# The delta rule's solve on TensorE: a block-diagonal state, two heads to one product

## The chip, the cores and the metric

One NeuronCore of a Trainium2 chip. The metric is device time of one launch in microseconds (us). The kernel before took 1455.86 us, the median of three runs (1449.7, 1455.86 and 1456.06).

## The reference, cut to what matters

A network of several blocks on 256 tokens in float32: feed-forward stages, mixers and gates. The change is inside one mixer, the `hyb` stage, which runs a stick-breaking attention (8 heads of 64) beside an RWKV-7 recurrence (8 heads of 64). Per head the recurrence is a delta rule with decay, over tokens t:

```
S_t = S_{t-1} * w_t  +  (S_{t-1} a_t) b_t^T  +  v_t k_t^T      (S is 64 x 64 for a head)
y_t = S_t r_t
```

The kernel computes it in two chunks of 128 tokens (c = 0, 1). With decays folded into A, R (queries of the removal and of the output), B and K (keys), it forms four 128 x 128 triangular matrices G for each head and chunk, and inverts (I - G0) in levels into Y. Then for each chunk:

```
right sides  rs = A S + G2 v          (S is zero in chunk 0, so the first term is left out there)
unknowns     us = Y rs
outputs      y  = R S + G1 us + G3 v
next state   S  = (B^T us + K^T v) * decay          (after chunk 0 only)
```

## The kernel before, in words

Each engine has its own instruction stream, written out by hand; an engine's instructions run in the order written, and semaphores (`signal(...)`, `.inc`, `.at`, `wait_ge`) order the engines among one another. Nothing is scheduled by a planner. `ps` is the PSUM tensor: 8 banks of 128 partitions x 512 float32. Everything in the solve is float32, and each float32 product appears in the profile as two records of MATMUL and two of LDWEIGHTS, so "x16" is eight products.

Two heads share a tile of 128 partitions: head 2j has partitions 0 to 63 and head 2j+1 partitions 64 to 127 of `AR[:, j]` (A and R, features first) and of the state `s0` (128 x 4 x 64). A product with the state therefore has 64 rows of stationary operand, `64*128` in the profile; products with G or Y have 128 rows, `128*128`.

TensorE's part of the solve (program order, after the seven levels of the inverse, L1393 to L1427):

- `rhs(0)` (L1365, eight products of 64 columns), `stick_scores(2)` (L1295, L1296), `unknowns(0)` (L1372), `stick_scores(3)`,
- `next_state` (L1379, L1380): for each head two products whose stationary operand has 64 columns, into partitions 0 to 63 or 64 to 127 of bank 7 (`128*64`),
- `outputs(0)` in two halves (L1388, L1389), `stick_sums(2)` between them (L1303, L1304, which wait for GpSimd's `softplus(2)`),
- a wait for the state and for the kept outputs of chunk 0, then `rhs(1)` in two halves (L1364 with the state, then L1365, for each head in turn), `stick_sums(3)` between and after them, `unknowns(1)`, `stick_out(2)` (L1313, L1314),
- `outputs(1)` two heads at a time (L1387 with the state, then L1388, L1389), each time followed by a quarter of the output gate: L1419 with 128 rows, L1420 with 32; `stick_out(3)` before the third quarter,
- `project_rows("hyb_out")` (L1034), four weight chunks; ahead of the third `turn_y` (L1433) transposes the normed outputs, and VectorE makes the second half of its input (L2713, L2716).

Even heads write bank 4 and odd heads bank 5, at columns `hd // 2 * 64`, for right sides and outputs alike. ScalarE keeps them with two ACTIVATEs of 256 columns (`keep_by_parity`, L1927) and the unknowns with one of 512 (L1932). VectorE makes the state from bank 7 with one instruction (L2687), ahead of `stick_softplus(2)` (L2660) in its queue; GpSimd masks what that makes (`softplus`, L2147). Later ScalarE, VectorE and GpSimd norm the outputs of each chunk (L2698 to L2705, L1947, L2101).

Weights come through six bays (L724); a bay is loaded again once TensorE has signalled that it is done with it. The gate's two chunks are released after L1420's last product, and their bays take the first weights of the next stage, `conv0`.

Of the kernel before, what the change touches and what calls it, by code (L numbers as in the profile page):

```python
# [11 lines left out]
ALU = mybir.AluOpType  # L12
ACT = mybir.ActivationFunctionType
AX = mybir.AxisListType

P = 128
# [201 lines left out]
def build(nc, I, scratch, out, book):  # L218
    new = {}
    ctx = ExitStack()  # L220
    with ctx:
        def sb(name, shape, dt=F32):
            return ctx.enter_context(nc.sbuf_tensor(name, shape, dt))

        def signal(name):
            return Signal(ctx, nc, name, book, new)
# [281 lines left out]
        at = at_k  # L508
        X, at = carve(at, 4, 4, P)
        Y, at = carve(at, 4, 4, P)  # L510
        rs, _ = carve(at - 2048 - 2048, 2, 4, 64)
        us, _ = carve(at - 2048 - 2048 + 512, 2, 4, 64)
        yv, _ = carve(at - 2048 - 2048 + 1024, 2, 8, 64)
        qaT, at = carve(at, 4, SEQ)
        kaT, at = carve(at, 4, SEQ)
# [6 lines left out]
        vtok = sq_flat[:, 0:1024].rearrange("p (t n) -> p t n", t=TT)  # L522
        bktok = sq_flat[:, 1024:2048]
        btok, ktok = bktok[:, 0:512], bktok[:, 512:1024]
        s0 = sb("state", [P, 4, 64])
        sfac = sb("state_decay", [P, 4])
        gmean = sb("group_mean", [P, 16])
        rw_in = signal("rwkv_projection_kept")
# [13 lines left out]
        sol_p = signal("solve_by_tensor")  # L542
        sol_a = signal("solve_by_scalar")
        sol_d = signal("solve_by_vector")
        LEVEL_N = len(LEVELS)
        STICK_BANK = [4, 6, 0, 2]

# [3 lines left out]
        def head(t, hd):  # L551

            return t[64 * (hd % 2):64 * (hd % 2) + 64, hd // 2]
# [212 lines left out]
        def _(pe):  # L766
            def weights(key, i=None):

                c = chunks[key]
                count = 16 * (c // BAYS + 1)  # L770
                pe.wait_ge(landed[c % BAYS].sem, count if i is None else i * 16 + count)
# [426 lines left out]
            def hyb():  # L1198
# [155 lines left out]
                level(5)  # L1354
                level(6)

                def cols64(b, hd):
                    return ps[:, b, hd // 2 * 64:hd // 2 * 64 + 64]

                def rhs(c, heads):  # L1360
                    for hd in heads:
                        o, vv = cols64(4 + hd % 2, hd), vtok[:, c, hd * 64:(hd + 1) * 64]
                        if c:
                            nc.tensor.matmul(o, head(AR, hd)[:, c, 0], head(s0, hd), start=True, stop=False)  # L1364
                        mm = nc.tensor.matmul(o, G[:, c, hd, 2], vv, start=(c == 0), stop=True)  # L1365
                    if 7 in heads:
                        mm.then_inc(*sol_p.inc("rhs", c))

                def unknowns(c):
                    pe.wait_ge(*sol_a.at("rhs", c))  # L1370
                    for hd in range(8):
                        mm = nc.tensor.matmul(ps[:, 6, (hd % 2 * 4 + hd // 2) * 64:(hd % 2 * 4 + hd // 2 + 1) * 64],  # L1372
                                              Y[:, c * 2 + hd // 4, hd % 4], rs[:, hd % 2, hd // 2], start=True, stop=True)
                    mm.then_inc(*sol_p.inc("u", c))

                def next_state():
                    for hd in range(8):
                        o = ps[64 * (hd % 2):64 * (hd % 2) + 64, 7, hd // 2 * 64:hd // 2 * 64 + 64]
                        nc.tensor.matmul(o, btok[:, hd * 64:(hd + 1) * 64], us[:, hd % 2, hd // 2], start=True, stop=False)  # L1379
                        mm = nc.tensor.matmul(o, ktok[:, hd * 64:(hd + 1) * 64], vtok[:, 0, hd * 64:(hd + 1) * 64], start=False, stop=True)  # L1380
                    mm.then_inc(*sol_p.inc("state"))

                def outputs(c, heads):
                    for hd in heads:
                        o = cols64(4 + hd % 2, hd)
                        if c:
                            nc.tensor.matmul(o, head(AR, hd)[:, c, 1], head(s0, hd), start=True, stop=False)  # L1387
                        nc.tensor.matmul(o, G[:, c, hd, 1], us[:, hd % 2, hd // 2], start=(c == 0), stop=False)  # L1388
                        mm = nc.tensor.matmul(o, G[:, c, hd, 3], vtok[:, c, hd * 64:(hd + 1) * 64], start=False, stop=True)  # L1389
                    if 7 in heads:  # L1390
                        mm.then_inc(*sol_p.inc("y", c))

# [9 lines left out]
                outputs(0, range(4, 8))  # L1402
                stick_sums(2, 1)
                pe.wait_ge(*sol_d.at("state"))
                pe.wait_ge(*sol_a.at("y", 0))
                rhs(1, range(4))
                stick_sums(3, 0)
                rhs(1, range(4, 8))
# [190 lines left out]
        def _(act):  # L1599
# [229 lines left out]
            def hyb():  # L1829
# [91 lines left out]
                level(5)  # L1921
                level(6)

                def keep_by_parity(dst, *event):
                    act.wait_ge(*sol_p.at(*event))
                    for n in range(2):
                        ins = nc.scalar.activation(dst(n), ps[:, 4 + n, 0:256].rearrange("p (a b) -> p a b", a=4), ACT.Copy)  # L1927
                    ins.then_inc(*sol_a.inc(*event))

                def keep_unknowns(c):  # L1930
                    act.wait_ge(*sol_p.at("u", c))
                    nc.scalar.activation(us[:].rearrange("p a b c -> p (a b c)"), ps[:, 6], ACT.Copy).then_inc(*sol_a.inc("u", c))  # L1932

                def keep_outputs(c):
                    keep_by_parity(lambda n: yv[:, c].rearrange("p (a b) e -> p b a e", b=2)[:, n], "y", c)

                keep_by_parity(lambda n: rs[:, n], "rhs", 0)
                stick_exponentials(2)
                keep_unknowns(0)
                stick_logs(2)  # L1940
# [8 lines left out]
                keep_by_parity(lambda n: rs[:, n], "rhs", 1)  # L1949
                squares_of_outputs(0)  # L1950
                stick_weights(3)
                keep_unknowns(1)
# [130 lines left out]
        def _(pool):  # L2083
# [45 lines left out]
            def hyb():  # L2129
# [75 lines left out]
        def _(dve):  # L2205
# [363 lines left out]
            def hyb():  # L2569
# [112 lines left out]
                for k in range(KD):  # L2682
# [222 lines left out]
```

## Time and profile before

| | us |
|---|---|
| median of three runs | 1455.86 |
| lowest, highest | 1449.70, 1456.06 |
| the profiled execution | 1451.71 |
| its span | 1450.0 |
| TensorE busy in it | 1391.6 |
| mean granted clock | 0.987 |

Times in the profile count from the span's start. PE is TensorE's matmuls, PEld its weight loads, DVE VectorE, ACT ScalarE, POOL GpSimd, SP SyncE; L1364 is line 1364 of the kernel. PEclk is the granted TensorE clock: 1.00 is 2.4 GHz, 0.50 is 1.2 GHz. A MATMUL's recorded duration contains its latency, so successive ones overlap; what one costs in a stream is read from starts, or from the chain of waits. The solve after the inverse stands between 811.7 and 854 us.

### The profile page before, as it was taken

The numbers are of one execution on the slowest core, as the hardware profiler recorded it, in microseconds if no ns is written. First come the engines' busy times: TensorE is split into PE (matmuls) and PEld (weight loads), VectorE is DVE, ScalarE is ACT, GpSimd is POOL, SyncE is SP. The second block draws the span as 40 slices with busy tenths as digits, with TensorE's granted clock in tenths as the row PEclk, the third lists the DMA queues.
The fourth block names the chain that finished last, engine by engine and source line by source line (L and its number), as shares of the span: only waits on it lengthen the run. The fifth ranks groups of instructions, "written<-read, shape, count | busy, mean of one in ns | idle before, by whom it ended". The sixth has DMA issues, their size and how long they took to land.

```text
span 1450.0 us, 25626 instructions
## 1 busy us (share of the span) xinstructions
PE 1391.6 (96%) x10812; PEld 1322.6 (91%) x10812; DVE 896.5 (62%) x1191; ACT 612.0 (42%) x727; POOL 158.9 (11%) x149
## 2 busy tenths in 40 slices
PE   8999999899999999999999999999989999999997
PEld 8999999798899999888889879999988778999997
DVE  5766676674357665732485417877776774777675
ACT  5443454443134554421323522444454473444444
POOL 0000001141000000601020010000051060000023
PEclk9999999999999999999999979999999999999998
DMA  8555745332345555433410024555543503555530
GB/s 340 186 192 198 244 162 189 121 128 77 145 174 175 202 196 188 167 105 111 151 62 1 2 87 159 183 188 197 202 146 115 201 1 117 175 204 189 191 142 29
DMA packets 34744, 218.99 MB, mean 151 GB/s; under 512 B 4259, under 2 KB 6732, under 8 KB 9452
## 3 DMA queue, kind: packets, MB, share of 16 engines
q1 hardware_dynamic: 31888, 215.59, 41.9%
q10 hardware_dynamic: 2780, 2.30, 0.5%
q8 instruction: 58, 0.95, 0.3%
q14 instruction: 18, 0.15, 0.0%
HBM read 216.68 MB, written 1.06 MB: 150 GB/s over the span
## 4 chain that ended last, share of the span: by engine, by line
PE 81%; DVE 10%; ACT 3%; issue 2%; POOL 1%; DMA 1%; SPq 0%; ACTq 0%; POOLq 0%; DVEq 0%
PE ps L894 35%; PE ps L943 14%; PE ps L1034 6%; PE ps L847 6%; PE ps L1016 2%; DVE weights_second_parts L2330 2%; PE ps L1323 2%; PE ps L1328 1%; PE ps L859 1%; DVE x_second_part L2224 1%; PE ps L831 1%; PE ps L1105 1%; PE ps L1005 1%; ACT weights_first_parts L1641 1%; DMA weight_bays<-in_ffn_in 1%
## 5 line engine op out<-in xcount | busy, mean ns | idle before, releaser
L2330 DVE TENSOR_TENSOR weights_second_parts<-weight_bays,weights_first_parts 128x2048 fp32r<-128x2048 f32 x130 | 296.7, 2289 | 151.2 <-ACT weights_first_parts L1641 151.0
L1641 ACT ACTIVATE weights_first_parts<-weight_bays 128x2048 fp32r<-128x2048 f32 x130 | 249.1, 1924 | 260.9 <-PE ps L894 170.0
L894 PE MATMUL ps<-x_first_part,weights_first_parts 128*128 128x256 f32 x1472 | 197.2, 277 | 4.3 <-DVE weights_second_parts L2330 3.7
L894 PE MATMUL ps<-x_second_part,weights_first_parts 128*128 128x256 f32 x1472 | 196.2, 276 | 0.0
L894 PE MATMUL ps<-x_first_part,weights_second_parts 128*128 128x256 f32 x1472 | 196.0, 276 | 0.0
L894 PEld LDWEIGHTS ps<-x_first_part,weights_first_parts 128*128 128x128 f32 x1472 | 180.1, 192 | 5.7 <-ACT weights_first_parts L1641 2.6
L894 PEld LDWEIGHTS ps<-x_second_part,weights_first_parts 128*128 128x128 f32 x1472 | 180.8, 193 | 0.0
L894 PEld LDWEIGHTS ps<-x_first_part,weights_second_parts 128*128 128x128 f32 x1472 | 180.7, 192 | 0.0
L943 PE MATMUL ps<-hidden_first_part,weights_first_parts 128*128 128x256 f32 x704 | 136.5, 276 | 10.1 <-ACT weights_first_parts L1641 7.5
L943 PE MATMUL ps<-hidden_first_part,weights_second_parts 128*128 128x256 f32 x704 | 136.2, 275 | 0.0
L943 PE MATMUL ps<-hidden_second_part,weights_first_parts 128*128 128x256 f32 x704 | 136.1, 275 | 0.0
L2126 POOL TENSOR_TENSOR weights_second_parts<-weight_bays,weights_first_parts 128x512 fp32r<-128x512 f32 x48 | 68.3, 1457 | 508.1 <-ACT weights_first_parts L1804 508.1
L943 PEld LDWEIGHTS ps<-hidden_first_part,weights_first_parts 128*128 128x128 f32 x704 | 106.8, 192 | 11.1 <-issue 6.1
L943 PEld LDWEIGHTS ps<-hidden_first_part,weights_second_parts 128*128 128x128 f32 x704 | 106.9, 192 | 0.0
L943 PEld LDWEIGHTS ps<-hidden_second_part,weights_first_parts 128*128 128x128 f32 x704 | 106.9, 192 | 0.0
L847 PE MATMUL ps<-xT,weight_bays 128*128 128x256 f32 (+1 forms) x368 | 80.8, 380 | 1.1 <-DVE xT L2294 1.1
L847 PEld LDWEIGHTS ps<-xT,weight_bays 128*128 128x128 f32 (+1 forms) x368 | 68.2, 186 | 12.7 <-ACT embedding L1783 1.3
L1034 PE MATMUL ps<-arena,weight_bays 128*128 128x256 f32 x320 | 69.9, 380 | 3.3 <-DVE arena L2513 1.5
L1034 PEld LDWEIGHTS ps<-arena,weight_bays 128*128 128x128 f32 x320 | 60.6, 190 | 12.3 <-DVE arena L2513 1.9
L2101 POOL TENSOR_TENSOR rstd<-mean_squares,minus_half 128x2 f32<-128x2 f32 (+2 forms) x17 | 15.3, 902 | 483.0 <-DVE mean_squares L2281 396.1
L1657 ACT ACTIVATE arena<-arena 128x512 f32<-128x512 f32 x22 | 14.0, 635 | 92.6 <-DVE arena L2349 92.6
L1629 ACT ACTIVATE arena<-arena 128x512 f32<-128x512 f32 x22 | 13.9, 630 | 68.1 <-DVE arena L2375 68.1
(429 smaller groups left out, 2191.1 us busy)
## 6 DMA issues: line engine op xcount, KB each, us to landing
weight_bays<-in_conv_in SPq DMA_DIRECT2D x44, 1024.0 KB, 4.7
weight_bays<-in_ffn_in SPq DMA_DIRECT2D x42, 1024.0 KB, 4.8
weight_bays<-in_ffn_out SPq DMA_DIRECT2D x22, 1024.0 KB, 4.8
weight_bays<-in_conv_out SPq DMA_DIRECT2D x22, 1024.0 KB, 4.7
weight_bays<-in_mix_in SPq DMA_DIRECT2D x19, 1024.0 KB, 4.8
weight_bays<-in_hyb_in SPq DMA_DIRECT2D x13, 1024.0 KB, 4.8
weight_bays<-in_ple_gate SPq DMA_DIRECT2D x12, 1024.0 KB, 4.7
weight_bays<-in_mix_out SPq DMA_DIRECT2D x4, 1024.0 KB, 5.3
```

What stands on the lines that cost most here:

```text
L831: mm = nc.tensor.matmul(ps[:, b0 + q, j % 2 * SEQ:(j % 2 + 1) * SEQ], w[:, k, j * P:(j + 1) * P], pT[:, n, k], start=(k == 0), stop=(k == 1))
L847: mm = nc.tensor.matmul(dst, lhs(k), xT[:, k] if rhs is None else rhs(k), start=(k == 0), stop=(k == n - 1), **kw)
L859: nc.tensor.matmul(dst[j], w[:, k, j * P:(j + 1) * P], xs[0][:, k], start=(k == 0 and w is hi and not (one_bank and j)), stop=False, skip_ ...
L894: mm = nc.tensor.matmul(dst, w[:, k, j * P:j * P + width], x[:, k], start=(n + k == 0), stop=(n == 2 and k == KD - 1))
L943: mm = nc.tensor.matmul(ps[:, tile // 2, tile % 2 * SEQ:(tile % 2 + 1) * SEQ], w[:, j, tile * P:(tile + 1) * P], in_halves(x[:, g % 2, j]) ...
L1016: mm = nc.tensor.matmul(ps[:, b0 + j // 2, j % 2 * SEQ:(j % 2 + 1) * SEQ], w[k // 2][:, k % 2, j * P:(j + 1) * P], srcT[:, k], start=(k == ...
L1034: mm = nc.tensor.matmul(ps[:, tile // 2, tile % 2 * SEQ:(tile % 2 + 1) * SEQ], w[:, j, tile * P:(tile + 1) * P], srcT(k) if callable(srcT) ...
L1323: mm = nc.tensor.matmul(ps[:, g, i * P:(i + 1) * P], G[:, g // 2, g % 2 * 4 + i, 0], X[:, g, i], start=True, stop=True)
L1641: nc.scalar.activation(hi, raw, ACT.Copy).then_inc(*w_hi_ready.inc(f, g, kind, of - g))
L2101: nc.gpsimd.tensor_tensor(rstd[:, c], msq[:, c], minus_half[:, c], ALU.pow).then_inc(*rstd_ready.inc(*n))
L2126: ins = nc.gpsimd.tensor_tensor(lo[:, part], raw[:, part], hi[:, part], ALU.subtract)
L2330: v.tensor_tensor(lo, raw, hi, ALU.subtract).then_inc(*w_lo_d.inc(f, g, kind, of - g))
```

## The change

The state becomes block-diagonal: `s0` is 128 x 4 x (2 x 64), with head 2j's 64 x 64 block at the upper left of tile j, head 2j+1's at the lower right, and zeros elsewhere, which GpSimd writes once (into the arena, where the inverse's M1 lay; hence its wait for the last level). One product of 128 rows and 128 columns, `from_state`, then serves two heads. Right sides go to bank 4 and outputs to bank 5 with all eight heads side by side, unknowns to bank 6 in the heads' order. Only the first product into a bank has `start=True`. `next_state` takes two heads as stationary operand and two as moving one: 128 x 128 results, of which only the two diagonal blocks are used; VectorE takes them with two instructions of 64 partitions. Each ACTIVATE pair becomes one of 512 columns. The wait for the kept outputs of chunk 0 moves from ahead of `rhs(1)` to ahead of the gate and `outputs(1)`.

```
-        rs, _ = carve(at - 2048 - 2048, 2, 4, 64)
-        us, _ = carve(at - 2048 - 2048 + 512, 2, 4, 64)
+        rs, _ = carve(at - 2048 - 2048, 8, 64)
+        us, _ = carve(at - 2048 - 2048 + 512, 8, 64)
+        s0, _ = carve(14080, RWT, 2, 64)
-        s0 = sb("state", [P, 4, 64])
...
+                def from_state(b, c, n, j):
+                    nc.tensor.matmul(ps[:, b, of_pair(j)], AR[:, j, c, n], s0[:, j].rearrange("p a d -> p (a d)"), start=(j == 0), stop=False,
+                                     skip_group_check=True)
 
                 def rhs(c, heads):
                     for hd in heads:
-                        o, vv = cols64(4 + hd % 2, hd), vtok[:, c, hd * 64:(hd + 1) * 64]
-                        if c:
-                            nc.tensor.matmul(o, head(AR, hd)[:, c, 0], head(s0, hd), start=True, stop=False)
-                        mm = nc.tensor.matmul(o, G[:, c, hd, 2], vv, start=(c == 0), stop=True)
+                        if c and hd % 2 == 0:
+                            from_state(4, c, 0, hd // 2)
+                        mm = nc.tensor.matmul(ps[:, 4, of_head(hd)], G[:, c, hd, 2], vtok[:, c, of_head(hd)], start=(c + hd == 0), stop=True,
+                                              skip_group_check=True)
...
                 def next_state():
-                    for hd in range(8):
-                        o = ps[64 * (hd % 2):64 * (hd % 2) + 64, 7, hd // 2 * 64:hd // 2 * 64 + 64]
-                        nc.tensor.matmul(o, btok[:, hd * 64:(hd + 1) * 64], us[:, hd % 2, hd // 2], start=True, stop=False)
-                        mm = nc.tensor.matmul(o, ktok[:, hd * 64:(hd + 1) * 64], vtok[:, 0, hd * 64:(hd + 1) * 64], start=False, stop=True)
+                    for j in range(RWT):
+                        o = ps[:, 7, of_pair(j)]
+                        nc.tensor.matmul(o, btok[:, of_pair(j)], us[:, 2 * j:2 * j + 2].rearrange("p a d -> p (a d)"), start=(j == 0), stop=False,
+                                         skip_group_check=True)
+                        mm = nc.tensor.matmul(o, ktok[:, of_pair(j)], vtok[:, 0, of_pair(j)], start=False, stop=True, skip_group_check=True)
...
                 def outputs(c, heads):
                     for hd in heads:
-                        o = cols64(4 + hd % 2, hd)
-                        if c:
-                            nc.tensor.matmul(o, head(AR, hd)[:, c, 1], head(s0, hd), start=True, stop=False)
+                        o = ps[:, 5, of_head(hd)]
+                        if c and hd % 2 == 0:
+                            from_state(5, c, 1, hd // 2)
...
                 pe.wait_ge(*sol_d.at("state"))
-                pe.wait_ge(*sol_a.at("y", 0))
                 rhs(1, range(4))
...
                 pe.wait_ge(*sol_a.at("u", 1))
+                pe.wait_ge(*sol_a.at("y", 0))
                 weights("g2")
...  (ScalarE)
+                def keep_rhs(c):
+                    act.wait_ge(*sol_p.at("rhs", c))
+                    nc.scalar.activation(rs.rearrange("p a b -> p (a b)"), ps[:, 4], ACT.Copy).then_inc(*sol_a.inc("rhs", c))
...  (GpSimd, between weights(1) and softplus(2))
+                pool.wait_ge(*inv_p.at("Y", LEVEL_N - 1, 3))
+                nc.gpsimd.memset(s0, 0.0).then_inc(*sol_g.inc("zero"))
...  (VectorE)
-                v.tensor_tensor(s0[:], ps[:, 7, 0:256].rearrange("p (a b) -> p a b", a=4), sfac[:].unsqueeze(2).to_broadcast([P, 4, 64]),
-                                ALU.mult).then_inc(*sol_d.inc("state"))
+                dve.wait_ge(*sol_g.at("zero"))
+                for n in range(2):
+                    r = slice(64 * n, 64 * n + 64)
+                    made = ps[r, 7].rearrange("p (j a d) -> p j a d", j=RWT, a=2)[:, :, n]
+                    ins = v.tensor_tensor(s0[r, :, n], made, sfac[r].unsqueeze(2).to_broadcast([64, RWT, 64]), ALU.mult)
+                ins.then_inc(*sol_d.inc("state"))
```

## Rows read from the trace of the kernel before

**Rows 1.** The page: engines; granted clock in 40 slices; the last chain by engine.

```profile
PE 1391.6 (96%) x10812; PEld 1322.6 (91%) x10812; DVE 896.5 (62%) x1191; ACT 612.0 (42%) x727; POOL 158.9 (11%) x149
...
PEclk9999999999999999999999979999999999999998
...
PE 81%; DVE 10%; ACT 3%; issue 2%; POOL 1%; DMA 1%; SPq 0%; ACTq 0%; POOLq 0%; DVEq 0%
```

**Rows 2.** Windows: stretch, length, busy per engine, PEclk, DMA share, GB/s.

```profile
817.24:818.37 1.13, 1.13 (x34) 1.06 (x32) 0.00 (x0) 1.13 (x1) 0.00 (x0) 1.00 0.00 0
824.98:827.75 2.77, 2.74 (x16) 2.30 (x17) 2.67 (x8) 1.99 (x2) 1.56 (x4) 1.00 0.00 0
828.80:831.55 2.75, 2.75 (x17) 2.27 (x16) 0.00 (x0) 0.00 (x0) 0.00 (x0) 1.00 0.02 6
835.26:837.02 1.76, 1.76 (x14) 1.55 (x13) 0.88 (x1) 0.38 (x1) 1.56 (x3) 1.00 0.00 0
837.02:838.28 1.26, 1.26 (x7) 0.60 (x6) 0.00 (x0) 0.00 (x0) 0.00 (x0) 1.00 0.00 0
840.93:854.18 13.25, 13.25 (x43) 8.49 (x42) 1.24 (x3) 1.04 (x3) 0.00 (x0) 0.50 0.00 0
854.18:857.94 3.76, 3.76 (x10) 3.04 (x10) 1.28 (x4) 0.63 (x1) 1.64 (x1) 0.50 0.66 220
```

**Rows 3.** The chain of waits in time order: start, us, what held it.

```profile
811.93 1.73 PE ps L1365 x16
...
823.83 0.22 PE ps L1389 x2
...
834.53 0.59 PE ps L1313 x4
835.12 0.22 PE ps L1314 x4
...
854.25 15.85 PE ps L1034 x64
...
872.30 7.82 PE ps L1034 x35
```

**Rows 4.** Timeline, TensorE: start, us, engine, line, tiles, shapes, records, [idle before].

```profile
808.20 3.74 PE L1328 MATMUL ps<-arena 128*128 128x128 f32 x32
...
825.70 0.43 PE L1364 MATMUL ps<-state,arena 64*128 64x64 f32 x2
826.07 0.43 PE L1365 MATMUL ps<-squares,arena 128*128 128x64 f32 x2
```

**Rows 5.** Timeline: from the state to the next product that waits.

```profile
818.48 0.42 DVE L2687 TENSOR_TENSOR state<-ps,state_decay 128x256 f32<-128x256 f32 x1 [2.65 <-PE ps L1380]
...
819.34 0.96 DVE L2660 SCALAR_TENSOR_TENSOR arena<-ps,arena 128x768 f32<-128x768 f32 x1 [0.43 <-ACT arena L1892]
...
821.19 0.91 PE L1303 MATMUL ps<-arena,mats 128*128 128x384 f32 x2 [0.82 <-POOL arena L2147]
...
825.38 0.87 POOL L2147 TENSOR_SCALAR_AFFINE_SELECT arena<-arena 128x256 f32<-128x256 f32 x2 [4.24 <-DVE arena L2660]
```

**Rows 6.** Timeline: GpSimd's clearing of 2048 columns, and its last mask.

```profile
735.88 1.81 POOL L2141 MEMSET arena<- 128x2048 f32 x1
...
835.60 1.22 POOL L2147 TENSOR_SCALAR_AFFINE_SELECT arena<-arena 128x256 f32<-128x256 f32 x2
```

**Rows 7.** Timeline: ScalarE's keeps of right sides and of unknowns.

```profile
831.82 0.66 ACT L1927 ACTIVATE arena<-ps 128x256 f32<-128x256 f32 x2 [4.83 <-PE ps L1365]
...
834.57 0.60 ACT L1932 ACTIVATE arena<-ps 128x512 f32<-128x512 f32 x1 [0.87 <-PE ps L1372]
```

**Rows 8.** Timeline: behind the solve, what is late next.

```profile
857.83 0.69 DVE L2705 TENSOR_TENSOR arena<-arena,rstd 128x512 f32<-128x512 f32 x1 [1.75 <-POOL rstd L2101]
...
873.68 6.69 DVE L2330 TENSOR_TENSOR weights_second_parts<-weight_bays,weights_first_parts 128x2048 fp32r<-128x2048 f32 x3
...
886.03 0.46 PE L859 MATMUL ps<-x_first_part,weights_first_parts 128*128 128x256 f32 x1
```

More of the change, by code:

```diff
@@ L544, in build @@
         sol_d = signal("solve_by_vector")
+        sol_g = signal("solve_by_gpsimd")
         LEVEL_N = len(LEVELS)
@@ L1355, in hyb, with of_pair, of_head @@
                 level(6)
-                def cols64(b, hd):
-                    return ps[:, b, hd // 2 * 64:hd // 2 * 64 + 64]
+                def of_pair(j):
+                    return slice(j * P, (j + 1) * P)
+                def of_head(hd):
+                    return slice(hd * 64, (hd + 1) * 64)
+                def from_state(b, c, n, j):
+                    nc.tensor.matmul(ps[:, b, of_pair(j)], AR[:, j, c, n], s0[:, j].rearrange("p a d -> p (a d)"), start=(j == 0), stop=False,
+                                     skip_group_check=True)
                 def rhs(c, heads):
                     for hd in heads:
-                        o, vv = cols64(4 + hd % 2, hd), vtok[:, c, hd * 64:(hd + 1) * 64]
-                        if c:
-                            nc.tensor.matmul(o, head(AR, hd)[:, c, 0], head(s0, hd), start=True, stop=False)
-                        mm = nc.tensor.matmul(o, G[:, c, hd, 2], vv, start=(c == 0), stop=True)
+                        if c and hd % 2 == 0:
+                            from_state(4, c, 0, hd // 2)
+                        mm = nc.tensor.matmul(ps[:, 4, of_head(hd)], G[:, c, hd, 2], vtok[:, c, of_head(hd)], start=(c + hd == 0), stop=True,
+                                              skip_group_check=True)
                     if 7 in heads:
@@ L1371, in unknowns @@
                     for hd in range(8):
-                        mm = nc.tensor.matmul(ps[:, 6, (hd % 2 * 4 + hd // 2) * 64:(hd % 2 * 4 + hd // 2 + 1) * 64],
-                                              Y[:, c * 2 + hd // 4, hd % 4], rs[:, hd % 2, hd // 2], start=True, stop=True)
+                        mm = nc.tensor.matmul(ps[:, 6, of_head(hd)], Y[:, c * 2 + hd // 4, hd % 4], rs[:, hd], start=(hd == 0), stop=True,
+                                              skip_group_check=True)
                     mm.then_inc(*sol_p.inc("u", c))
                 def next_state():
-                    for hd in range(8):
-                        o = ps[64 * (hd % 2):64 * (hd % 2) + 64, 7, hd // 2 * 64:hd // 2 * 64 + 64]
-                        nc.tensor.matmul(o, btok[:, hd * 64:(hd + 1) * 64], us[:, hd % 2, hd // 2], start=True, stop=False)
-                        mm = nc.tensor.matmul(o, ktok[:, hd * 64:(hd + 1) * 64], vtok[:, 0, hd * 64:(hd + 1) * 64], start=False, stop=True)
+                    for j in range(RWT):
+                        o = ps[:, 7, of_pair(j)]
+                        nc.tensor.matmul(o, btok[:, of_pair(j)], us[:, 2 * j:2 * j + 2].rearrange("p a d -> p (a d)"), start=(j == 0), stop=False,
+                                         skip_group_check=True)
+                        mm = nc.tensor.matmul(o, ktok[:, of_pair(j)], vtok[:, 0, of_pair(j)], start=False, stop=True, skip_group_check=True)
                     mm.then_inc(*sol_p.inc("state"))
@@ L1384, in outputs @@
                     for hd in heads:
-                        o = cols64(4 + hd % 2, hd)
-                        if c:
-                            nc.tensor.matmul(o, head(AR, hd)[:, c, 1], head(s0, hd), start=True, stop=False)
-                        nc.tensor.matmul(o, G[:, c, hd, 1], us[:, hd % 2, hd // 2], start=(c == 0), stop=False)
-                        mm = nc.tensor.matmul(o, G[:, c, hd, 3], vtok[:, c, hd * 64:(hd + 1) * 64], start=False, stop=True)
+                        o = ps[:, 5, of_head(hd)]
+                        if c and hd % 2 == 0:
+                            from_state(5, c, 1, hd // 2)
+                        nc.tensor.matmul(o, G[:, c, hd, 1], us[:, hd], start=(c + hd == 0), stop=False, skip_group_check=True)
+                        mm = nc.tensor.matmul(o, G[:, c, hd, 3], vtok[:, c, of_head(hd)], start=False, stop=True, skip_group_check=True)
                     if 7 in heads:
@@ L1922, in hyb @@
                 level(6)
[L1924 to L1928, printed above, removed]
+                def keep_rhs(c):
+                    act.wait_ge(*sol_p.at("rhs", c))
+                    nc.scalar.activation(rs.rearrange("p a b -> p (a b)"), ps[:, 4], ACT.Copy).then_inc(*sol_a.inc("rhs", c))
                 def keep_unknowns(c):
                     act.wait_ge(*sol_p.at("u", c))
-                    nc.scalar.activation(us[:].rearrange("p a b c -> p (a b c)"), ps[:, 6], ACT.Copy).then_inc(*sol_a.inc("u", c))
+                    nc.scalar.activation(us.rearrange("p a b -> p (a b)"), ps[:, 6], ACT.Copy).then_inc(*sol_a.inc("u", c))
                 def keep_outputs(c):
-                    keep_by_parity(lambda n: yv[:, c].rearrange("p (a b) e -> p b a e", b=2)[:, n], "y", c)
-                keep_by_parity(lambda n: rs[:, n], "rhs", 0)
+                    act.wait_ge(*sol_p.at("y", c))
+                    nc.scalar.activation(yv[:, c].rearrange("p a b -> p (a b)"), ps[:, 5], ACT.Copy).then_inc(*sol_a.inc("y", c))
+                keep_rhs(0)
                 stick_exponentials(2)
@@ L1947, in squares_of_outputs @@
                     nc.scalar.activation(ysq[:, c], yv[:, c], ACT.Square).then_inc(*sol_a.inc("squares", c))
-                keep_by_parity(lambda n: rs[:, n], "rhs", 1)
+                keep_rhs(1)
                 squares_of_outputs(0)
```

## The prediction

> **What bounds the kernel now.** I read the page first: TensorE is busy for 1391.6 of 1450.0 us and holds 81% of the chain that ended last, while the next engine, VectorE, is at 62% [rows 1]. So time that leaves TensorE's stream leaves the kernel, unless a wait takes its place. The line of the granted clock has one slice that stands out, a 7 between 834 and 870 us, and that is where the edited code runs. The windows then resolve the solve: until 840.9 us the clock is 1.00; from 840.93 to 857.94 it is 0.50, half rate, although TensorE is busy in all of both stretches [rows 2]. The chain of waits lies on TensorE almost throughout, and it gives what a product costs in a stream: eight products of 64 columns with G take 1.73 us, 0.22 each, and so does a single one in the outputs [rows 3]. The timeline gives two more prices. 16 products of 128x128 by 128 columns take 3.74 us less one latency, again 0.22: a stationary operand of 128 columns costs the same with 64 or with 128 moving columns [rows 4]. And where 64-row products alternate with 128-row ones, each start is 0.37 us behind the last instead of 0.22 [rows 4]: 0.14 to 0.15 us is lost at each change of height.
>
> **Next state: dearer.** Now 16 products with 64-column stationary operands run from 817.24 to 818.37, 1.13 us, or 0.07 each (its x34 are their 32 records and two of the tail ahead) [rows 2]. The new one is 8 products of 128x128 by 128 columns at 0.22: 1.79 us, so +0.65. The least it could be is equal (a change of shape before the outputs falls away, 0.15), the most 8 x 0.37 = 2.9 us, +1.8. VectorE's one instruction of 0.42 us [rows 5] becomes two with the same number of elements per partition on half the partitions: between +0 (both at half the price) and +0.42; I take +0.38, since the elements per partition set the time of all its rows here. The state is then ready near 819.95 instead of 818.91. It stands in VectorE's queue ahead of the second pair's softplus, which began at 819.34 when ScalarE's logarithm came; that moves to about 819.95, and with it GpSimd's mask and the product that waits for it, at 821.19 after 0.82 us of idling [rows 5]. TensorE's own extra 0.65 us falls into that idle time. Cost on the path: **+0.6 us** (bounds 0 and +1.8).
>
> The Trainium skill has a rule that speaks against this edit: "TensorE: Matmul & The Clock Gate", Part 3, says that products of few rows or columns should be placed in different strips of the array, where they run at once. By that rule giving up the 64-column form costs up to half of the throughput here. The trace agrees for next_state, where the 64-column ones stood together (0.07 against 0.22), and the sum above already holds it; for the 64-row ones with the state it has nothing to give, since each stands between two of full height.
>
> **Right sides of chunk 1.** Now two stretches of eight products, 824.98 to 827.75 and 828.80 to 831.55: 5.5 us [rows 2]. New: 4 + 8 products of full height at 0.22, 2.7 us. With the height change into each stretch: **-3.0 us**. Bounds: -1.1 if each still cost 0.37 (12 x 0.37 = 4.4), and -3.2.
>
> **Outputs of chunk 1.** At full clock two heads take 1.76 us (six products, changes of height around the state's) [rows 2]; the new five products take 1.12. Four such: **-2.6 us**. Bounds -0.0 (5 x 0.37 = 1.85 each) and -2.8. The gate's quarters, 1.26 us with a 32-row product that keeps its two changes of height, stay [rows 2].
>
> **The clock.** Before it fell TensorE did just this alternation: 64-row products of 64 columns between full ones, and 32-row products of the gate, all with pauses. It rose again in the dense hyb_out stream [rows 2]. The earlier alternating stretch of the right sides, with the dense sums between, kept 1.00 [rows 2]. The new outputs have neither the 64-row products nor their pauses, and one product in five streams 128 columns; what is left of pauses is two per gate quarter. They are denser than both old stretches, the one that kept the clock too, so I take it that the clock stays. Its worth, by the new stream at full clock: from 835.26 to 854.18 the kernel now needs 18.9 us; new 4 x (1.12 + 1.26) + 0.85 for the last attention product (0.59 + 0.22 and a change [rows 3]) = 10.4 us. That is -8.6, of which -2.6 is counted above: **-6.0 us**. Then the 32 products of hyb_out ahead of the transposes take 15.85 us now; in the second half they run at 7.82 / 35 = 0.2234 us a record, 64 of them in 14.3: **-1.5 us** [rows 3]. Bounds of the clock's part: 0 and -7.5; more in executions in which the clock now falls earlier than in this one.
>
> The skill's same page ("Why this matters for your kernels") ties a throttled clock to idle gaps between bursts of products; [rows 2] show a fall with TensorE never idle. By the page's rule nothing in this change would touch the clock, and the sum would be the first rival's.
>
> **What costs nothing, and its cover.** GpSimd's clearing of 512 columns: 2048 took 1.81 us [rows 6], so 0.45 us (at most 1.8); it can run from 812 on and the next one who needs GpSimd or the zeros comes at 818.5. Cover gone, it is its own 0.45. ScalarE's pair of 0.66 us becomes one of 512 columns, 0.60 [rows 7]; the keep of the right sides is beside the last sums, so nothing, and as little for the outputs. The moved wait: outputs of chunk 0 were kept about when TensorE came, so 0 to -0.2, taken as 0; at its new place the keep is some 7 us old. With a faster TensorE its partners could be late. The softplus mask of the last pair is done at 825.38 + 0.87 = 826.25 [rows 5]; TensorE, started at 825.6 with six products, comes at 826.9: cover 0.7 us, the thinnest here. The right sides' keep is again beside 0.9 us of sums. The last weights' mask stands in GpSimd's queue behind the norm of chunk 0, and that hangs on ScalarE's keep of the new right sides: now the keep ends at 832.48 [rows 7] and the mask at 836.82 [rows 6], 4.3 us later; new the keep ends near 829.8, so the mask near 834.2, and the product that needs it comes at 838. The normed outputs of chunk 1 are ready at 858.5 [rows 8] for transposes at 870.1 [rows 3]; both move. Behind that the loads for conv0 start with the gate's release, so they move along; their parts are split at 880.4, for a first product at 886.03 [rows 8]: 5.6 us of cover, of which 1.5 goes.
>
> **Sum**, against the profiled execution's 1451.71: +0.6 - 3.0 - 2.6 - 6.0 - 1.5 = -12.5, giving 1439.2. The profiled execution lies 4.15 below the median of the runs, 1455.86, from which the same sum gives 1443.4. What separates those runs I can't see; if it is how long the clock was low, the gain is larger in the slow ones. I forecast **1442 us**, chance 0.72, own range 1435 to 1446.
>
> **Rivals.**
>
> *The clock falls all the same* (or falls late in the stretch), chance 0.15. For it: the gate's 32-row products and their pauses stay, and they were in the stretch where it fell. Against: the right sides above. Then only +0.6 - 3.0 - 2.6 = -5.0 is left, 1450.9; with a late fall a few of the 7.5 are kept. I price it 1449, 1445 to 1451.
>
> *The loss isn't one of height.* If every product that follows another operand of another tensor costs 0.37, the bounds above give +1.8 - 1.1 - 0.0 = about +0.7, and some of the clock: 1450 to 1456, chance 0.05. Against: L1388 and L1389 alternate between tensors at 0.22 [rows 3]. This is also the case in which the change doesn't do what it says.
>
> *Slower: the pause ahead of the first sums drops the clock early.* TensorE idles 0.82 us there now [rows 5]; new about 1.0, since the mask comes 0.6 later and outputs(0) start 0.65 later. If the clock fell there and came back only in hyb_out, the new 21 us from 821.8 to 842.9 would take about 18 us more (waits and pauses don't double), and hyb_out 1.5: 1443.4 + 19.5 = 1463. It makes the kernel slower if more than the 12.5 us won are lost, that is if the low stretch begins before about 830. Against: the idle time is nearly the same and dense sums follow it at once. Chance 0.05; the remaining 0.03 is for sizes outside all of these.
>
> **Range and chances.** 0.5%, 7.3 us, is about what a measurement of this kernel can tell from no change. Faster by more than that needs 1448.6 or less: nearly all of 0.72 and half of the first rival's 0.15, and the better half of the rest's: 0.84. Within: 0.11. Slower: 0.05. The 8-in-10 range takes the forecast's own and the first rival's: 1434 to 1451.
>
> **What would show it.** A granted clock of 1.00 from the outputs into hyb_out (rival one: 0.50 in some window there); starts 0.22 us apart in the right sides of chunk 1, two halves of 1.3 us; two heads' outputs in 1.1 us; next_state 1.8 us long and the first sums 0.6 us later against their predecessors; VectorE's state in two instructions near 0.4 us; no idle TensorE before the last pair's sums. The prediction is wrong if the clock is at half rate in the new stretch, or if a new wait for GpSimd's masks stands ahead of the sums or the attention products.

## The result, and the profile after

The changed kernel takes 1441.51 us (median of six, 1440.45 to 1443.64) against 1455.96 for the kernel before (six, 1449.70 to 1456.44). The ratio is 0.9907, 95% interval 0.9894 to 0.9920: 14.45 us faster. The forecast was 1442, range 1434 to 1451.

The profiled execution took 1441.73 us with a span of 1440.0, 10.0 less than before. Windows of the changed kernel (columns as in [rows 2]), answering to [rows 2] and the 15.85 us of [rows 3]:

```profile
819.69:824.51 4.82, 3.78 (x34) 3.64 (x32) 1.80 (x3) 4.78 (x5) 0.77 (x2) 1.00 0.00 0
828.03:829.37 1.34, 1.34 (x15) 1.34 (x14) 1.31 (x4) 1.33 (x2) 0.65 (x2) 1.00 0.00 0
830.24:831.58 1.34, 1.34 (x15) 1.34 (x14) 0.50 (x1) 0.00 (x0) 1.12 (x2) 1.00 0.00 0
835.22:836.33 1.11, 1.11 (x12) 1.11 (x11) 0.70 (x1) 0.38 (x1) 1.11 (x3) 1.00 0.00 0
836.33:837.59 1.26, 1.26 (x7) 0.60 (x6) 0.17 (x1) 0.00 (x0) 0.43 (x1) 1.00 0.00 0
835.22:845.65 10.43, 10.43 (x67) 7.41 (x65) 1.25 (x2) 1.36 (x3) 1.54 (x3) 1.00 0.00 0
845.65:859.57 13.92, 13.92 (x66) 12.22 (x66) 2.72 (x6) 6.26 (x4) 1.64 (x1) 1.00 0.61 227
```

The two halves of the right sides of chunk 1 take 1.34 us each (2.77 and 2.75 before), two heads' outputs 1.11 (1.76), a gate quarter 1.26 as before, all outputs with the gate 10.43 instead of 18.92. PEclk is 1.00 in every one of them, where it was 0.50 for 17 us. hyb_out runs 13.92 us up to its transposes (15.75).

The timeline of the changed kernel, all engines, answering to [rows 5, 6]:

```profile
814.21 1.90 PE L1372 MATMUL ps<-squares,arena 128*128 128x64 f32 x16
...
814.44 0.52 POOL L2172 MEMSET arena<- 128x512 f32 x1 [33.21 <-PE ps L1329]
...
819.69 0.49 PE L1387 MATMUL ps<-arena,squares 128*128 128x128 f32 x2
...
821.58 0.33 PE L1397 MATMUL ps<-arena 128*128 128x64 f32 x2
...
821.77 0.86 DVE L2701 TENSOR_TENSOR arena<-ps,state_decay 64x256 f32<-64x256 f32 x2 [3.49 <-PE ps L1389]
...
822.66 0.96 DVE L2670 SCALAR_TENSOR_TENSOR arena<-ps,arena 128x768 f32<-128x768 f32 x1
...
823.69 0.77 POOL L2155 TENSOR_SCALAR_AFFINE_SELECT arena<-arena 128x256 f32<-128x256 f32 x2 [8.73 <-DVE arena L2670]
...
824.51 0.91 PE L1304 MATMUL ps<-arena,mats 128*128 128x384 f32 x2 [1.04 <-POOL arena L2155]
```

Here is the one part that got dearer. next_state lasts 1.89 us (819.69 to 821.58; 1.13 before), VectorE's two state instructions 0.86 (0.42), and the softplus, which had waited for a logarithm, now follows VectorE's own state at once. From next_state's first product to the first sums it is 4.82 us instead of 3.95. The clearing of the zeros, 0.52 us at 814.44, is in nobody's way.

One measure serves for all kernels below: **the solve**, from the start of chunk 0's first right side to the start of hyb_out's first product, and **the tail**, from there to the start of the transposes. Before: 811.77 to 854.18 and to 869.93, 42.41 and 15.75 us. After: 814.21 to 845.65 and to 859.57, 31.44 and 13.92. Together -12.80. The other 2.8 us of the span's -10.0 went the other way, outside the change: the solve began 2.44 us later, because ahead of the solve the clock fell in places where it hadn't in that execution of the kernel before. These are windows of the changed kernel:

```profile
35.00:40.00 5.00, 3.79 (x20) 3.82 (x21) 4.90 (x5) 1.64 (x3) 0.00 (x0) 0.67 0.51 201
450.00:455.00 5.00, 5.00 (x31) 5.00 (x32) 4.82 (x3) 2.90 (x2) 0.00 (x0) 0.68 0.35 149
610.00:615.00 5.00, 5.00 (x32) 5.00 (x30) 2.54 (x2) 0.00 (x0) 5.00 (x5) 0.66 0.13 23
```

In the kernel before, PEclk is 1.00 in all three of these stretches (it has a fall of its own between 625 and 635 us). Such falls come and go from one execution to the next, so two single executions can't be subtracted; the medians and the local stretches can.

### The profile page after: what moved, and what is told of

Same layout as the page of the kernel before. It is cut to its first block, busy times and chain, and to the rows that moved or that the text cites. A ratio compares the mean times of both kernels' runs of the same rounds, so it can differ in the third digit from the quotient of the medians.

```text
span 1440.0 us, 25560 instructions
## 1 busy us (share of the span) xinstructions
PE 1384.3 (96%) x10780; PEld 1320.8 (92%) x10780; DVE 897.1 (62%) x1192; ACT 611.1 (42%) x723; POOL 159.6 (11%) x150
## 4 chain that ended last, share of the span: by engine, by line
PE 84%; DVE 8%; ACT 3%; issue 2%; POOL 2%; ACTq 0%; POOLq 0%; DVEq 0%
PE ps L895 36%; PE ps L944 15%; PE ps L1035 6%; PE ps L848 6%; PE ps L1017 2%; PE ps L1324 2%; PE ps L1329 1%; PE ps L832 1%; PE ps L860 1%; POOL weights_second_parts L2134 1%; DVE x_second_part L2234 1%; PE ps L1106 1%; ACT weights_first_parts L1650 1%; PE ps L1006 1%; PE ps L1496 1%
```

## The experiments

All medians stand beside medians of the kernel before between 1455.8 and 1456.2 us, measured along with each. The ratio isn't the quotient of the two medians; how sure a difference is, its interval tells.

| kernel | median us (runs) | ratio to before, 95% | solve | tail | low clock in them |
|---|---|---|---|---|---|
| before | 1455.96 (6) | | 42.41 | 15.75 | 840.9 to 857.9 |
| before, again | 1459.41 (1) | | 43.39 | 16.40 | 841.7 to 862.2 |
| after | 1441.51 (6) | 0.9907 (0.9894 to 0.9920) | 31.44 | 13.92 | none |
| after, again | 1441.34 (6) | 0.9896 (0.9875 to 0.9917) | 34.72 | 13.92 | 825.4 to 832.2 |
| outputs by head | 1454.29 (12) | 0.9990 (0.9975 to 1.0005) | 41.27 | 15.98 | 840.3 to 860.7 |
| right sides by head | 1453.57 (12) | 0.9962 (0.9934 to 0.9990) | 46.17 | 16.80 | 835.8 to 866.5 |
| by head, grouped | 1444.46 (6) | 0.9926 (0.9904 to 0.9948) | 32.32 | 13.92 | none |
| before with filler | 1450.65 (12) | 0.9979 (0.9958 to 1.0000) | 39.98 | 13.92 | none |
| before, tails together | 1453.85 (12) | 0.9996 (0.9974 to 1.0018) | 41.94 | 15.41 | 840.8 to 857.8 |
| tails together | 1440.31 (6) | 0.9900 (0.9869 to 0.9930) | 30.17 | 13.82 | none |
| narrow state | 1441.20 (1) | | 30.79 | 13.91 | none |
| both edits | 1438.56 (6) | 0.9894 (0.9863 to 0.9924) | 29.52 | 13.82 | none |
| best | 1439.01 (6) | 0.9911 (0.9872 to 0.9949) | 28.23 | 13.81 | none |
| best, again | 1438.29 (6) | 0.9884 (0.9860 to 0.9908) | 28.24 | 13.81 | none |

The last columns are of the one profiled execution; the ends of a low stretch are read from windows of 1 us.

### The outputs undone

(`by_parity(hd)` is a head's old place: bank 4 for even heads, bank 5 for odd ones.)

```
-                        if c and hd % 2 == 0:
-                            from_state(5, c, 1, hd // 2)
+                        nc.tensor.matmul(by_parity(hd), head(AR, hd)[:, c, 1], s0[64 * (hd % 2):64 * (hd % 2) + 64, hd // 2, hd % 2], start=True, stop=False)
```

> The changed kernel with only the outputs of chunk 1 as before: eight state products of 64 rows, each between products of 128 rows, even heads in bank 4 and odd ones in bank 5. My theory (the changes of height cost 0.14 us each, and their pauses, together with the gate's 32-row products, are what drops the clock): two heads' outputs back from 1.11 to 1.76 us, +2.6 us in all, and a granted clock of 0.50 from somewhere in the outputs into hyb_out, +6 to +7.5: 1450 to 1452 us. Rival (the fall of the clock has nothing to do with the state products' pauses, the change only happened to miss it): +2.6 alone, 1444 us, clock 1.00 in that stretch.

Measured: 1454.29 us, nearly all of the gain gone. Windows of that kernel, the first pair of heads and the low stretch:

```profile
836.26:838.07 1.81, 1.81 (x15) 1.61 (x13) 0.88 (x1) 0.38 (x1) 1.55 (x3) 1.00 0.00 0
840.40:856.52 16.12, 16.12 (x51) 10.58 (x51) 1.24 (x3) 1.04 (x3) 0.00 (x0) 0.50 0.00 0
856.52:860.75 4.23, 4.23 (x11) 3.42 (x11) 1.75 (x4) 0.63 (x1) 1.64 (x1) 0.50 0.72 261
```

Two heads cost 1.81 us again and the clock falls 4 us into the outputs. The fall is tied to the old form of the outputs; the rival is out. The edit brings back the two banks and the two ACTIVATEs too; the grouped kernel below has both of them and kept 1.00, which leaves the products between full ones. It lasted longer than in the kernel before, so the time lies 2 to 4 us above what I expected.

### The right sides undone

```
-                        if c and hd % 2 == 0:
-                            from_state(4, c, 0, hd // 2)
+                        nc.tensor.matmul(by_parity(hd), head(AR, hd)[:, c, 0], s0[64 * (hd % 2):64 * (hd % 2) + 64, hd // 2, hd % 2], start=True, stop=False)
```

> The changed kernel with only the right sides of chunk 1 as before (64-row state products between full ones, two banks, the wait for the kept outputs back ahead of them). My theory: each half back from 1.34 to 2.76 us, +2.9 us in all, clock at 1.00 through the outputs: 1444.5 us. Rival (the clock depends on how sparse the whole solve is, not on the outputs with the gate): the clock falls as in the kernel before, 1451 us.

A miss, and the most telling run. The 12 runs are of two kinds: six between 1442.6 and 1449.6, as I expected, and six between 1457.5 and 1466.3, above the kernel before. The median, 1453.57, lies in the gap between them, where no run is, and the ratio leaves the longest run (1466.27) out. The profiled one (1458.96) is of the second kind; its windows:

```profile
828.48:831.29 2.81, 2.81 (x18) 2.34 (x17) 2.40 (x6) 1.89 (x2) 1.28 (x4) 1.00 0.00 0
832.30:835.12 2.82, 2.82 (x18) 2.35 (x17) 0.00 (x0) 0.00 (x0) 0.00 (x0) 1.00 0.00 0
835.12:835.90 0.78, 0.78 (x5) 0.48 (x5) 0.00 (x0) 0.58 (x3) 0.00 (x0) 0.92 0.00 0
835.90:860.62 24.72, 24.72 (x92) 17.90 (x90) 3.04 (x6) 3.37 (x7) 2.81 (x3) 0.50 0.00 1
860.62:866.50 5.88, 5.88 (x15) 4.71 (x15) 1.80 (x4) 0.63 (x1) 1.64 (x1) 0.50 0.79 297
```

The clock falls right behind the by-head right sides, and then stays at 0.50 through the new, full-height outputs: from 841.21 to 860.62 they take 19.4 us, the same instructions that take 10.43 us in the changed kernel at 1.00. So these outputs can keep a high clock high, but didn't bring a low one back in 19.4 us.

### By head, but grouped

The right sides' part; in the outputs all eight state products stand ahead of the first pair.

```
+                    for hd in heads:
+                        nc.tensor.matmul(by_parity(hd), head(AR, hd)[:, c, 0], s0[64 * (hd % 2):64 * (hd % 2) + 64, hd // 2, hd % 2], start=(hd < 2), stop=False, skip_group_check=True)
+                    for hd in heads:
+                        mm = nc.tensor.matmul(by_parity(hd), G[:, c, hd, 2], vtok[:, c, of_head(hd)], start=False, stop=True, skip_group_check=True)
```

> No block-diagonal product at all: 64-row state products of single heads as before, but standing together (four in a row ahead of each half of the right sides, all eight ahead of the outputs), even heads in bank 4, odd ones in bank 5. My theory (it is the changes of height that cost, not the number of products): 64-row products of alternating halves in a row cost 0.11 to 0.15 us each, so the right sides' half takes about 1.6 us instead of 1.34 and the outputs' stretch about as long as in the changed kernel; clock 1.00; 1442 to 1443 us. Rival (the merging of two heads into one product is what pays): eight products at 0.22 or more, +2 us and more, 1444 to 1446, and 1452 if the clock falls.

Measured: 1444.46 us, with a solve of 32.32, 0.9 over the changed kernel's. The timeline (TensorE) of the grouped kernel:

```profile
829.27 0.66 PE L1382 MATMUL ps<-arena 64*128 64x64 f32 x8
829.86 1.10 PE L1384 MATMUL ps<-squares,arena 128*128 128x64 f32 x8
...
834.45 1.11 PE L1415 MATMUL ps<-arena 64*128 64x64 f32 x16
835.49 0.43 PE L1417 MATMUL ps<-arena 128*128 128x64 f32 x2
```

Eight 64-row products of alternating halves take 1.04 us, 0.13 each, where each took 0.37 between full ones. It is the alternation of heights that cost, and in this execution grouping gives back nearly all that the block-diagonal state gives. It is the shortest of the six, though (1441.12). The median is 3 us above the changed kernel's, its interval overlaps (0.9904 to 0.9948 against 0.9894 to 0.9920), and three of the runs lie between 1446.1 and 1450.8; whether the clock fell in their solve, no trace shows.

### More work in the kernel before

```
                     outputs(1, range(2 * n, 2 * n + 2))
+                    nc.tensor.matmul(ps[:, 1], ident, vtok[:, 0], start=True, stop=True, skip_group_check=True)
```

> The kernel before with four products more, which nobody reads: identity (128x128) by 512 columns into the free bank 1, one behind each pair of heads in the outputs of chunk 1. Each costs about 0.9 us of TensorE at full clock, 3.6 in all. My theory (sparse products dropped the clock): with the stream denser there the clock stays at 1.00 in the outputs, so 1456 + 3.6 - 7.5 = 1452 us: faster with more work. Rival (the fall isn't made by how TensorE is used there): 1460 us, or 1463 with the fillers at half clock.

Measured: 1450.65 us against 1456.03, so not slower with four products more. That it is faster is at the edge of the noise: the ratio's interval, 0.9958 to 1.0000, reaches 1. The profiled execution is the shortest of the twelve, and four of them lie between 1454.7 and 1455.5. What the trace shows is the clock at 1.00 throughout. Its windows, one filler, then the whole of the outputs, then the tail:

```profile
837.61:838.52 0.91, 0.91 (x4) 0.44 (x4) 0.00 (x0) 0.00 (x0) 0.00 (x0) 1.00 0.00 0
835.80:852.29 16.49, 16.49 (x83) 10.53 (x81) 1.98 (x4) 1.43 (x4) 1.55 (x3) 1.00 0.00 0
852.29:866.21 13.92, 13.92 (x66) 12.21 (x66) 2.00 (x4) 6.26 (x4) 1.64 (x1) 1.00 0.61 227
```

This divides the gain, by the local stretches of three single executions. Without fillers and without a fall the old solve would be 39.98 - 4 x 0.91 = 36.34 us. The fall cost 42.41 - 36.34 = 6.1 in the solve and 15.75 - 13.92 = 1.8 in the tail, 7.9; the products' shape gave 36.34 - 31.44 = 4.9.

### Which part of the outputs drops it

The kernel before with the gate's four 32-row products in a row ahead of the outputs:

```
+                for j in range(4):
+                    nc.tensor.matmul(ps[:, 6 + j // 2, j % 2 * SEQ:(j % 2 + 1) * SEQ], wt[:, j * P:(j + 1) * P], xm[0:32, 14],
+                                     start=(j % 2 == 0), stop=False, skip_group_check=True)
```

> The kernel before with only the gate's four 32-row products in a row ahead of the outputs of chunk 1; its state products stay 64 rows high between full ones. It tells the gate's share in the fall of the clock from the state products'. My theory (the state products' pauses suffice): the clock still falls in the outputs, 1454 to 1455 us, only the six changes of height less at half clock. Rival (the gate's small products were needed for the fall): 1.00 in the outputs, 1456 - 7.5 - 0.9 = 1447.5 us.

Measured: 1453.85 us, and 0.50 from 840.8 to 857.8. A window of this kernel, from the fall to hyb_out:

```profile
840.80:854.59 13.79, 13.79 (x50) 10.54 (x50) 0.03 (x1) 1.04 (x3) 0.00 (x0) 0.50 0.00 0
```

So the gate's small products needn't stand between full ones for the fall; the state products do. The small ones still stand in a row ahead of them here, but the same row ahead of the merged outputs ("A better version") left the clock at 1.00.

### The kernel before, once more

> The kernel before once more, to see where the clock falls in another execution. My theory: always within the right sides or outputs of chunk 1, which of the two varies; the earlier it falls, the longer the execution (up to 1460 us; where it doesn't fall, about 1446). Rival (it always falls in the outputs, and the executions differ elsewhere): the fall at the same place within 3 us, relative to the first right side.

It fell in the outputs again, 28.0 us behind the first right side (29.1 in the first profile): the rival's "within 3 us" holds. But the low stretch lasted 20.5 us, not 17, and the two stretches together 59.79 us instead of 58.16. Against the changed kernel's 45.36 that is -14.4. A window of this execution, the low stretch up to hyb_out:

```profile
841.70:857.10 15.40, 15.40 (x49) 9.98 (x49) 1.25 (x3) 1.04 (x3) 0.00 (x0) 0.50 0.00 0
```

The other half of the rival, that executions differ elsewhere, holds as well: the span is 7.7 us longer than in the first profile (1457.7 against 1450.0), and only 1.6 of that lies in solve and tail. My half about the right sides wasn't seen in this kernel; it was seen only with the outputs changed, above.

### The changed kernel, once more

> The changed kernel once more, beside the version with all three edits: 1441.5 us, with no slow tail (1440 to 1444), since in no execution should the clock fall in the solve; the kernel before 1456.

1441.34 us confirms the time, but "in no execution" is refuted. Timeline and then a window of this execution:

```profile
823.29 0.39 PE L1398 MATMUL ps<-squares,arena 128*128 128x64 f32 x2
824.72 1.06 PE L1304 MATMUL ps<-arena,mats 128*128 128x384 f32 x2 [1.05 <-POOL arena L2155]
```

```profile
825.65:832.40 6.75, 6.75 (x30) 6.14 (x29) 3.85 (x8) 3.99 (x5) 0.93 (x3) 0.52 0.00 0
```

TensorE waits 1.05 us for GpSimd's mask, and just behind that the clock is at 0.50; it is back at 832.2, within the new right sides. The solve took 34.72 us instead of 31.44.

### A better version

Three edits on top of the change. First the gate's small products together, as above:

> The changed kernel, with the gate's four 32-row products (128 sigmoid features are in one product, the last 32 in this one) taken out of the quarters and put in a row ahead of the outputs of chunk 1; the full products then add to them. My theory (a change of height costs 0.14 to 0.16 us wherever it is): eight changes become two, a quarter's gate goes from 1.26 to 0.45 us, the four small ones take 1.8 us in a row; -0.9 us in all, and pauses fewer still, so the clock stays at 1.00: 1440.6 us. Rival (four products of 32 rows in a row are the sparsest work of all and drop the clock): 0.50 in the outputs, as in the kernel with the right sides by head, 1455 us.

Solve 30.17 (-1.27; -0.9 expected, so six changes less gave 0.21 each and not 0.15): a quarter's gate product no longer stands between changes of height. In a row the four take 1.9 us (836.39 to 838.31), and the clock stays at 1.00. Then next_state in its old shape, into the diagonal blocks only:

```
+                        o = ps[64 * (hd % 2):64 * (hd % 2) + 64, 7, of_head(hd)]
+                        nc.tensor.matmul(o, btok[:, of_head(hd)], us[:, hd], start=(hd < 2), stop=False, skip_group_check=True)
...
```

> Only next_state in its old form on top of the changed kernel, for the trace. My theory: from the first product of next_state to the first sums 4.2 us instead of 4.8 (before: 3.95). Rival: 4.8, if VectorE's two instructions or the logarithm set it.

Window of this kernel, from next_state's first product to the first sums, 3.98 us (4.2 expected) against 4.82 with two heads to a product:

```profile
819.97:823.95 3.98, 3.13 (x51) 2.93 (x49) 1.80 (x3) 3.95 (x4) 0.77 (x2) 1.00 0.00 0
```

> The same and next_state in its old form of 64-column stationary operands, written into the diagonal blocks only: 16 products in 1.13 us instead of 8 in 1.79. My theory: VectorE's state 0.65 us earlier, the second pair's softplus 0.6 earlier, and with it GpSimd's mask and the first sums; -0.6 us more on top of -0.9: 1440.0 us. Rival: the first sums wait for the chain of ScalarE's logarithm anyhow, 0 for this part.

Solve 29.52, 1438.56 us. And with outputs(0) and rhs(1) no longer cut in halves by the sums, so that four heads' outputs fill the wait for the mask:

```
-                outputs(0, range(4))
+                outputs(0, range(8))
                 stick_sums(2, 0)
-                outputs(0, range(4, 8))
...
-                rhs(1, range(4))
+                rhs(1, range(8))
                 stick_sums(3, 0)
-                rhs(1, range(4, 8))
```

> The version with both edits (gate's small products in a row, next_state in its old form), and now all eight heads' outputs of chunk 0 ahead of the second pair's sums, and all eight heads' right sides of chunk 1 ahead of the last pair's. TensorE idles 1.0 us there now, waiting for GpSimd's mask; my theory: four heads' outputs (1.8 us) fill that idle time, first right side to hyb_out from 29.5 to 28.5 us, 1437.6 us. Rival: the masks come late everywhere, the wait only moves to the last pair's sums, 29.5 and 1438.5 us.

> All three edits again. First right side to hyb_out took 28.23 us against 31.44 in the changed kernel: if the rest of the kernel doesn't give it back, 1441.5 - 3.2 = 1438.3 us; rival: falls of the clock elsewhere take it back, 1441.

Windows of the best kernel: outputs of chunk 0 with both sums' start, the gate's small products, the tail.

```profile
821.44:826.85 5.41, 5.41 (x43) 4.88 (x41) 1.80 (x3) 5.34 (x7) 0.77 (x2) 1.00 0.00 0
833.90:835.82 1.92, 1.92 (x10) 1.40 (x9) 0.87 (x1) 0.38 (x1) 1.92 (x3) 1.00 0.00 0
843.07:856.88 13.81, 13.81 (x65) 12.11 (x64) 3.10 (x6) 6.56 (x5) 1.64 (x1) 1.00 0.62 229
```

The six runs of "best" have their median at 1439.01 us where 1437.6 was expected; the solve of 28.23 is near the 28.5 expected. TensorE is busy in all 5.41 us; the idle time is gone. The solve is 28.23 and 28.24 us in two executions, 3.2 under the changed kernel's, and the medians side by side are 1438.29 and 1441.34. The intervals against the kernel before overlap (0.9860 to 0.9908 and 0.9875 to 0.9917), so the runs alone don't tell these two apart; nor do they tell "both edits" from "best". The traces do.

## Why the prediction was right

The forecast of 1442 us and the sum's local terms both held; the mechanism did too, with three reservations below. Measured on solve and tail against the profiled execution of before:

| step | predicted | measured |
|---|---|---|
| next state, to the first sums | +0.6 | +0.87 |
| right sides, with the changes into them | -3.0 | -2.84 in the two halves alone; -3.31 from the first sums to the unknowns (11.35 to 8.04 us) |
| outputs, shape alone | -2.6 (1.76 to 1.12 for two heads) | 1.76 to 1.11 |
| shape in all | -5.0 | -4.9 |
| clock in the outputs | -6.0 | -6.1 |
| clock in hyb_out | -1.5 | -1.8 |
| sum | -12.5 | -12.80 |

- **Next state** was the term furthest off: I took 1.79 us and 0.38 for VectorE; they measured 1.89 and 0.44 more. The cover I named, the idle time ahead of the sums, did hide TensorE's own part.
- **Changes of height.** The grouped kernel shows it apart: 0.13 instead of 0.37 us for the same products. The Trainium skill says: "Changing tiling mode (not just tile) drains the TensorE" ("TensorEngine Tiling (Array Packing)", Key Properties); the runs agree, with 0.14 to 0.15 us a change here by the starts. That price is low: it sets 0.22 us for a 64-row product, which in a row of its like costs 0.13, and the gate's six changes less gave 0.21 each. My second rival falls with it.
- **The clock.** The filler kernel and the one with the outputs undone confirm the mechanism and, with 7.9 us, its size. The Trainium skill's tie of a throttled clock to idle gaps ("TensorE: Matmul & The Clock Gate", "Why this matters for your kernels") isn't enough here: TensorE was busy throughout ahead of the falls at 840.9 [rows 2] and 835.8, and there denser work, not less idling, kept the clock up. Two small things in this term: 18.9 - 10.4 is 8.5 and not 8.6, and hyb_out's 64 records take 13.92 us at full clock, not 14.3, which is why its part is -1.8 and not -1.5.
- **One reason was weaker than it looked.** I took it as evidence that the old right sides had kept 1.00 [rows 2]. With only the outputs changed, the clock fell behind those same right sides in about half of the runs (if the longer kind is the same thing in all of them: one profile shows it, and the mean granted clock of the runs divides the same way, 0.974 to 0.980 against 0.985 to 0.991). The conclusion held because the change takes the alternation out of both places. With the outputs undone little is left, 1454.3 us; with the right sides undone half of the runs keep nearly all of the gain and half are longer than the kernel before.
- **The first rival** (the clock falls all the same) isn't what was measured in the outputs, in either of the two profiles of the changed kernel.
- **The slower rival** had a wrong price, and its mechanism stays open. The clock did drop behind the longer pause ahead of the first sums, in one of two profiled executions of the changed kernel. Four more kernels have a pause of 1.04 or 1.05 us there and kept 1.00 behind it in their profiles, so it isn't shown that the pause is the cause. And the clock came back within 7 us instead of staying low to hyb_out, so it cost 3.3 us and not 19.5.
- **The covers** held: no TensorE idling ahead of the last pair's sums, GpSimd's zeros 7 us early, and conv0's first product came 16.09 us behind the transposes (859.57 to 875.66), as before (869.93 to 886.03).
- **The median.** The sum from the profile gave 1439.2, from the median 1443.4, and 1442 was a choice between the two; that it lies 0.5 us from the measured 1441.51 is partly luck. Both starting points were off. Outside solve and tail the spans of the 14 profiled executions are between 1391.8 and 1397.9 us, 1394.4 in the middle, and before's first profile has the shortest, 1391.8. With 1394.4, and the 1.7 us by which a run is longer than its span, a run at before's median has 59.9 us for solve and tail, not 58.16, and one at the changed kernel's median 45.4. That is an estimate, but it accounts for both gaps: a longer low stretch than in the first profile makes -14.5 out of -12.8, and the other 2.6 of the 4.25 us by which that profile lies below the median stand outside the change.

What stays open: what in the stream the clock goes by. The runs only order streams: the alternation of heights drops it, the same with fillers didn't in its one profile, the merged and the grouped products didn't in theirs, but for the short fall of the changed kernel. How often each kernel falls isn't known from traces. The runs give a hint for the kernel before: 7 of its 75 runs beside these experiments lie between 1444.3 and 1448.4 us, where the estimate without a fall is 1394.4 + 1.7 + 36.34 + 13.92 = 1446.4. Beside such a run the change would gain some 5 us by this estimate, its shape alone.

## What to carry to other kernels

Look for float32 products of 64 or 32 rows that stand singly between full-height ones: each costs two changes of height, and in the profiled executions grouping them was worth nearly as much as merging them (32.32 and 31.44 us). Before such work is priced, look at the granted clock behind it: here more than half of the gain was the clock, it lasted far beyond the sparse stretch, and mending one of two sparse stretches gave almost nothing (the right sides) or the gain in only half of the runs (the outputs). A stretch that keeps its clock in one profile may lose it in the next, so repeat the profile before taking it as evidence.

## What the runs showed of the hardware that I had not expected

- More work didn't make the kernel slower, and probably made it faster: four unread products of 0.91 us each, 1450.65 against 1456.03 us, ratio 0.9979 (0.9958 to 1.0000). The stretch of solve and tail was 53.90 us instead of 58.16.
- The same instructions ran at two speeds for their whole length: the merged outputs 10.43 us when they began at 1.00, and 19.4 us when they began at 0.50. Dense hyb_out work brought the clock back only 3.2 to 5.9 us after its start in five profiles (854.59 to 857.8 at the least; 860.62 to 866.5 at the most).
- Four 32-row products in a row (1.92 us) didn't drop the clock, in four profiles with the merged outputs behind them.
